# A two-part transformer kernel on one Trainium2 core: its norms taken chunk by chunk

## The reference

```python
def rms_norm(x, g):
    y = x * rsqrt(mean(square(x), axis=-1) + EPS)      # EPS = 1e-6
    return y * g

for layer in range(2):
    h = rms_norm(x, norm_mix_g[layer])
    x = x + (mixer_ab if layer == 0 else mixer_rglru)(h, ...)
    h = rms_norm(x, norm_ffn_g[layer])
    x = x + hierarchical_moe(h, ...)
x = rms_norm(x, norm_final_g)
for i in range(2):
    x = x + attention(rms_norm(x, ln1_g_2[i]), ...)
    x = x + ffn(rms_norm(x, ln2_g_2[i]), ...)
return rms_norm(x, final_g_2)
```

## Time and profile before

| | us |
|---|---|
| median of 3 runs | 2907.57 |
| lowest, highest | 2907.46, 2908.96 |
| the profiled execution, by its own time | 2907.38 |
| its span in the trace | 2906.1 |
| mean granted clock of TensorE | 0.952 |
| busy: PE, PEld, DVE, ACT, POOL | 2752.5, 1905.8, 1198.4, 898.2, 358.9 |

### The profile page before, as it was taken

The page is one execution under the profiler, slowest core; times in us unless marked ns, Lnnn a source line. Parts: engine busy times, 40 slices in busy tenths (PEclk is TensorE's granted clock), DMA queues, the critical chain, the costliest instruction groups (busy, mean ns, idle before and its releaser), DMA issues. The chain is left out here.

```text
span 2906.1 us, 36407 instructions
## 1 busy us (share of the span) xinstructions
PE 2752.5 (95%) x14944; PEld 1905.8 (66%) x14944; DVE 1198.4 (41%) x2253; ACT 898.2 (31%) x1596; POOL 358.9 (12%) x197
## 2 busy tenths in 40 slices
PE   7988999999878899999979999999999999999998
PEld 5874445444656544544467767788887776788887
DVE  2543223223645222322236652552443674245254
ACT  3431111111463110111154543442334454343233
POOL 3200000000330000000020011222122001122112
PEclk9989999999988999999989978999999996899999
DMA  5147999998315799999822011223231201123312
GB/s 201 61 177 302 398 405 406 396 406 340 102 44 195 293 401 408 403 401 405 320 76 73 30 59 44 79 96 102 73 107 56 75 16 58 44 87 103 101 59 80
DMA packets 134825, 543.60 MB, mean 187 GB/s; under 512 B 14592, under 2 KB 26112, under 8 KB 85376
## 3 DMA queue, kind: packets, MB, share of 16 engines
q1 hardware_dynamic: 126976, 536.41, 47.8%
q10 hardware_dynamic: 7680, 4.81, 0.6%
HBM read 539.09 MB, written 2.10 MB: 186 GB/s over the span
## 5 line engine op out<-in xcount | busy, mean ns | idle before, releaser
L484 PE MATMUL ps<-w,w 128*128 128x512 f32 x3360 | 771.0, 391 | 16.4 <-DVE w L430 9.1
L484 PEld LDWEIGHTS ps<-w,w 128*128 128x128 f32 x3360 | 634.2, 189 | 150.6 <-DVE w L430 9.7
L256 POOL TENSOR_TENSOR w<-w,w 128x1024 fp32r<-128x1024 f32 (+3 forms) x139 | 330.2, 2384 | 2294.9 <-ACT w L248 2294.9
L486 PE MATMUL ps<-w,w 128*128 128x512 f32 (+2 forms) x2256 | 498.9, 383 | 27.0 <-ACT w L556 16.0
L486 PEld LDWEIGHTS ps<-w,w 128*128 128x128 f32 x2256 | 417.8, 192 | 105.8 <-ACT w L556 16.3
L1124 PE MATMUL ps<-w,w 128*64 128x512 f32 x2048 | 451.6, 594 | 1.8 <-issue 1.8
L248 ACT ACTIVATE w<-w 128x1024 fp32r<-128x1024 f32 (+3 forms) x260 | 252.6, 1001 | 481.0 <-PE ps L484 254.8
L256 DVE TENSOR_TENSOR w<-w,w 128x1024 fp32r<-128x1024 f32 (+3 forms) x121 | 180.7, 1498 | 456.1 <-ACT w L248 454.3
L1124 PEld LDWEIGHTS ps<-w,w 128*64 128x64 f32 x2048 | 145.9, 137 | 285.5 <-issue 285.5
L1356 DVE TENSOR_TENSOR X<-ps,X 128x512 f32<-128x512 f32 x256 | 164.1, 683 | 222.0 <-PE ps L1160 221.1
L1146 PE MATMUL ps<-w,w 128*64 128x512 f32 x1024 | 226.8, 595 | 0.8 <-ACT w L1201 0.8
(11 more groups left out here) (231 smaller groups left out, 2296.4 us busy)
## 6 DMA issues: line engine op xcount, KB each, us to landing
w<-in_moe_w_gate SPq DMA_DIRECT2D x128, 1024.0 KB, 10.2
w<-in_moe_w_up SPq DMA_DIRECT2D x128, 1024.0 KB, 12.8
w<-in_moe_w_down SPq DMA_DIRECT2D x128, 1024.0 KB, 8.0
w<-in_w_up SPq DMA_DIRECT2D x40, 1024.0 KB, 5.1
w<-in_w_down SPq DMA_DIRECT2D x20, 1024.0 KB, 5.0
w<-in_w_in SPq DMA_DIRECT2D x16, 1024.0 KB, 5.0
w<-in_ab_w_in SPq DMA_DIRECT2D x10, 1024.0 KB, 6.5
w<-in_c_w_in SPq DMA_DIRECT2D x8, 1024.0 KB, 5.3
```

The costliest lines, as they stand in the source:

```text
L256: up(self.wlo[self.low[s][0]], lane.e.tensor_tensor(lo, raw, hi.bitcast(F32), ALU.subtract))
L484: ins = pe.matmul(bank[:, :], wp[:, k, P * o:P * o + P], ap(k0 + k), start=first, stop=stop)
L486: ins = pe.matmul(bank[:, 0:width], ap(k0 + k)[:, P * o:P * o + P], wp[:, k, :], start=first, stop=stop)
```

## The change

The change takes each norm in smaller pieces and starts it earlier:

- the squares of a stage's last product are summed by column halves (`scalar_last_product`): the first half of all four chunks during the last product, the second half behind each chunk's last addition, with a root for each chunk; the sum of the first half enters the root as its bias;
- VectorE scales each chunk behind the next chunk's addition (`vector_last_product`), in the stage before, and the last chunk in two halves; in `moe(0)` two chunks are scaled ahead of chunk 3's additions, in `moe(1)` none;
- the scaled rows lie in fixed places (`XN_`, `HF_`), free at that time;
- TensorE takes the banks of the transposes one by one, so that it waits for each only where it writes it, and waits for halves of chunk 3;
- `tensor_product` runs over input blocks outside and banks inside, and waits for each block by itself;
- the gain of the middle norm comes with the weight units (`plan_middle`), and ScalarE issues four small transfers for the attention at the start of the middle norm; the middle norm is a stage of its own;
- the roots at the start and at the end of the experts are for chunks 0 and 1, then 2, then 3;
- behind the experts only VectorE waits for the roots.

```diff
+    XN_ = (at(8192, 4, 1024), at(20480, 4, 1024))
...
+    def norm_of_rows(XN):
+        def apply(c):
+            if c == 0:
+                mark["xn"] = xn.n
+            w = D if c < NT - 1 else D // 2
+            for j in range(0, D, w):
+                up(xn, dve.tensor_scalar(XN[:, c, j:j + w], X[:, c, j:j + w], SM[:, c:c + 1], None, ALU.mult))
+        return apply
...
     def tensor_norm_features(XN):
-        bs = [banks.take(bf) for _ in range(KD)]
+        bs = []
         for chunks in (range(NT - 1), (NT - 1,)):
             for k in range(KD):
+                if not chunks[0]:
+                    bs.append(banks.take(bf))
                 for c in chunks:
-                    PE.wait_ge(xn, c + 1)
+                    PE.wait_total(xn, mark["xn"] + (c + 1 if c < NT - 1 else NT + k // (KD // 2)))
...
-            ready(k0 + nk)
             hi, lo = (x.rearrange("p (k n) -> p k n", k=nk) for x in W.need(s, PE))
-            for o, bank in zip(outs, bs):
-                for k in range(nk):
+            for k in range(nk):
+                ready(k0 + k + 1)
+                last = end and k == nk - 1
+                for o, bank in zip(outs, bs):
...
+    def scalar_last_product(key, tail):
+        done = len(bx.banks) - 2 * NT
+        steps = W.steps(key)
+        for i, (h, _, _) in enumerate(steps[:len(steps) - tail]):
+            W.hi(h + SPLITS)
+            if i == 0:
+                for c in range(NT):
+                    S.wait_total(bx.free, done + c + 1)
+                    square(X[:, c, 0:512], 512, SM[:, 88 + c:89 + c])
+                S.wait_total(sq, sq.n)
+                S.wait_total(ss, up(ss, act.activation(SM[:, 88:92], SM[:, 88:92], ACT.Identity, bias=ONE[:, 2:3],
+                                                       scale=1.0 / D)))
+        for c in range(NT):
+            S.wait_total(bx.free, done + NT + c + 1)
+            square(X[:, c, 512:D], 512, SM[:, c:c + 1])
+            scalar_roots(c, 1, D, SM[:, 88 + c:89 + c])
+
+    def vector_last_product(key, tail, apply):
+        steps = W.steps(key)
+        for h, _, _ in steps[:len(steps) - tail]:
+            W.lo(h + SPLITS, V)
+        for c in range(NT):
+            vector_add_chunk(1, c)
+            if c:
+                vector_norm(apply, ((c - 1, 1),))
+        vector_norm(apply, ((NT - 1, 1),))
...
+            for c in range(3):
+                vector_combine(c)
+            if next_norm:
+                vector_norm(next_norm, ((0, 2),))
+            vector_combine(3)
+            if next_norm:
+                vector_norm(next_norm, ((2, 1), (3, 1)))
...
         for lane in (PE, S, V, G, SP):
             lane.wait_ge(n_ready, 1)
-            lane.wait_ge(bx.free, 8 * PAIRS)
-            lane.wait_total(rt, rt.n)
-            lane.wait_ge(bdown.free, 2 * PAIRS)
+        V.wait_total(rt, rt.n)
...
+    def plan_middle():
+        W.add("fn", [(1, D, A["norm_final_g"].partition_broadcast(P).unsqueeze(1))], split=False)
```

More of the change, by code:

```diff
@@ L395, in vector_roots, with vector_norm @@
         vstep(dve.reciprocal(a, a))
-    def vector_norm(apply):
-        for c0, n in ((0, NT - 1), (NT - 1, 1)):
+    def vector_norm(apply, groups):
+        for c0, n in groups:
             vector_roots(c0, n)
@@ L487, in tensor_product @@
                                             start=first, stop=stop)
-                if end:
-                    W.consumed_at[s] = (kind.full, up(kind.full, ins))
+                    if last:
+                        W.consumed_at[s] = (kind.full, up(kind.full, ins))
             if not end:
@@ L571, in evacuate, with vector_add_chunk, vector_out @@
             for c in range(NT):
-                bank = bx.next(V)
-                x = X[:, c, 512 * n:512 * n + 512]
-                up(bx.free, dve.tensor_tensor(x, bank[:, :], x, ALU.add))
-        return evacuate
-    def vector_out(key):
-        for n in range(2):
-            vector_product((key, n), vector_add_to_x(n), TAIL * n)
+                vector_add_chunk(n, c)
+        return evacuate
+    def vector_add_chunk(n, c):
+        bank = bx.next(V)
+        x = X[:, c, 512 * n:512 * n + 512]
+        up(bx.free, dve.tensor_tensor(x, bank[:, :], x, ALU.add))
+    def vector_out(key, apply):
+        vector_product((key, 0), vector_add_to_x(0))
+        vector_last_product((key, 1), TAIL, apply)
     def scalar_squares(ready):
@@ L1367, in vector @@
             vector_route()
-            for p in range(PAIRS + 1):
-                now, before, after = p < PAIRS, p > 0, p + 1 < PAIRS
-                if before:
+            for p in range(PAIRS):
+                if p:
                     vector_combine(0)
-                if now:
-                    vector_hidden(p)
-                if before:
+                vector_hidden(p)
+                if p:
                     vector_combine(1)
                     vector_combine(2)
-                if after:
+                if p + 1 < PAIRS:
                     vector_gather(p + 1)
-                if now:
-                    vector_slots(p)
-                if before:
+                vector_slots(p)
+                if p:
                     vector_combine(3)
@@ L1849, in vector @@
         def vector():
-            vector_norm_features(gain, XN, late)
+            vector_norm_features(gain, late)
             vector_product(("mla", i))
@@ L2064, in vector @@
                 for n in range(2):
[L2065 removed]
+                    if m0 and n:
+                        vector_last_product(("fd", i, m0, n), FFN_TAIL, next_norm)
+                    else:
+                        vector_product(("fd", i, m0, n), vector_add_to_x(n))
         def gpsimd():
@@ L2112, in program @@
         plan_ffn(i)
-    def nothing():
-        pass
-    def load_fn_att():
-        load_final("norm_final_g")
-        load_att(0)
     sync_start()
```

173 lines of the change are left out of this document (95 added, 78 removed).

## The result

| us | before | changed kernel |
|---|---|---|
| median of the first timed runs | 2907.52 (4 runs) | 2878.59 (4 runs) |
| lowest, highest | 2901.32, 2908.96 | 2876.93, 2879.96 |
| span of the profiled execution | 2906.1 | 2875.7 |
| TensorE busy in it | 2752.5 | 2737.2 |
| TensorE idle in it (span less busy) | 153.6 | 138.5 |

The ratio is 0.9904, with a 95% interval of 0.9887 to 0.9921: 28.9 us faster, where 19.6 were forecast and 26.6 was the far end of the range. A second set of six runs of the changed kernel had a median of 2878.13, against 2908.34 for the kernel before on the same chip.

A forecast was written before the change was run, and what follows sets the result against it. TensorE was taken as the bound almost everywhere, leaving its idle time and matmul pace. Gains of 20.45 us, less 2.8 for bank order, plus 2.0 for the clock, gave 19.65, so 2888.0 us; range 2881 to 2897.

The forecast's parts named there:

- Dense seams: Three dense seams: only chunk 2's scaling remains behind the last addition, so transposes start 1.3 us earlier each, 3.9 together.
- Into the experts: Two seams into the experts: earlier scalings let TensorE restart 3.3 us sooner each, 6.6 together.
- Out of the first experts: Seam behind the first experts: two chunks scaled before chunk 3's additions, so the bulk of transposes starts 2.2 us earlier.
- Middle: Middle norm: the gain comes with the weight queue, its 5.16 us wait goes, and TensorE's bulk restarts 1.5 us earlier.
- End: Last norm: only chunks 2 and 3 remain to scale behind the last additions, 2.35 us gained.
- Start: Kernel's start: the first two chunks are scaled before the third's root, 1.35 us gained.
- Single features: Products wait for one feature, not two: three output products gain 0.65 us each, the recurrent one 0.6; sum 2.55.
- Order of banks: Narrow groups of two feed-forward stages: later banks delay GpSimd's low part, costing 1.4 us each, minus 2.8 together.
- (1): Rival, dense matmuls: more bank changes slow TensorE; over 22 ns each, chance 0.03; a 5 to 10 us loss, 0.07.
- (2): Rival, seams: lower-clock stretches stay as frequent and new waits open two more, 2890 to 2894 us; chance 0.2.
- (3): Rival: the clock gives +4 to +8 us and the narrow groups don't wait, 2880 to 2884 us; chance 0.1.
- The clock: Eight seams: shorter idling should leave fewer lower-clock stretches on TensorE, +2.0 us, bounds -4 and +8.

The follow-up runs named there:

- e9: Changed kernel with chunk 3's two additions at the end of moe(0) back ahead of the first two scalings: 2875.65 us.
- e7: Changed kernel with the middle norm's gain fetched by ScalarE's queue at the start of that norm instead of with the weights: 2881.80 us.
- e1: Changed kernel with products again running over banks outside and the step's two blocks inside, waiting for both blocks: 2881.16 us.
- e2: Changed kernel with only the last step of a product run bank by bank again, blocks outside in all other steps: 2876.51 us.
- the second pair: Changed kernel and kernel before, each traced once more without edits: 2878.13 us (6 runs) and one execution of 2903.99 us.
- e6: Changed kernel with VectorE's scalings behind all four last additions again at the two seams into the experts alone: 2888.84 us.
- e8: e2 with a product's banks taken one by one, each just ahead of its first matmul: 2859.70 us.
- e5: Changed kernel with VectorE's scalings behind all four last additions again at the three dense seams alone: 2886.76 us.
- e4: Changed kernel with scalings behind all four last additions again at the dense seams, the seams into the experts and the end: 2899.16 us.
- e10: Changed kernel with the edits of e8 and e9 together: 2856.32 us, 0.9835 of the kernel before.

## Why the prediction was wrong

The direction was right and the size was not: the time lies 2.4 us below the range. By the prediction's own steps, from the first pair of traces:

- *Dense seams.* Predicted 1.3 each; the bulk starts 2.95 - 1.61 = 1.34 earlier. Right.
- *Into the experts.* Predicted 3.3 each. Addition to restart took 8.45 and takes 193.40 - 188.55 = 4.85, so 3.6. Right, a little small.
- *Out of the first experts.* Predicted 2.2, measured 6.95 - 5.37 = 1.6. The two scalings ahead of chunk 3's additions took 2.31 us in place of the 1.42 that the earlier trace rows gave, and the additions waited behind them; e9 shows that this step of the change costs 1.2 us at its own seam. What is left of the gain I put down to the earlier root and the missing branch; no run parts the two. The step failed by pricing a move at the duration that the scaling had in another place: the first of the two began while GpSimd still made a low part. (The kernel before varies here: 6.95 in its first trace, 742.10 - 734.00 = 8.10 in its second.)
- *Middle.* Predicted 1.5, measured 14.68 - 12.59 = 2.1. All of it lies ahead of the reciprocal: from there to the bulk it takes 7.92 us where it took 7.87. The mechanism was right (e7, with the gain late, lost 3.7), the size 0.6 short: 0.3 because VectorE came 4.67 us behind the last matmul where I had 1464.1 - 1459.13 = 4.97, since the last root was 0.3 later and 0.67 passed behind it instead of the 1.3 taken over from the other experts' seam, and 0.3 because the scalings took 7.92 where I had 8.2.
- *End.* Predicted 2.35; 4.59 - 2.19 = 2.40. Right. *Start.* Predicted 1.35; the bulk starts at 13.76 against 15.26, so 1.5. Right.
- *Single features.* Predicted 2.55. The waits of features turned back fell by 2.0 and the recurrent one by 0.8, 2.8 together. Right as waits; e1 against e2 shows 4.7 in time.
- *Order of banks.* Predicted minus 1.4 in each narrow pair of ffn; 1.27 measured at the place and for the reason named, and e2 removes it. Right.
- *Rivals.* (1) A change of bank costs nothing that these rows show: 130.84 us for 576 matmuls with either order. (2) and (4) are out, the clock gave more and the seams moved as forecast. (3) comes nearest, but one of its two conditions did not hold: the narrow groups did wait.
- **The clock.** Predicted +2.0 with bounds of -4 and +8. Here is the failed step. TensorE is busy for 15.3 us less in the first pair of traces and for 4.6 us less in the second pair (2744.8 against 2740.2), so no single pair of traces measures it; their mean is 10.0. The times agree: 28.9 gained, of which the steps above explain 4.0 + 7.2 + 1.6 + 2.1 + 1.5 + 2.4 + 2.8 - 2.5 = 19.1. Some 10 us are left for the clock, above my upper bound. This is a difference of medians: against the three groups of the kernel before it would be some 4, 10 and 16.

The sum without the clock, 17.65, is thus right to 1.5 us, in part by luck: out of the first experts it was 0.6 too high, in the middle 0.6 too low. What I did with the clock was to treat it as chance: eight seams, each of which "could win or lose" a stretch, with a small mean. The mean is not small. Over fourteen traces a dense seam's window loses up to 1.4 us less when its idle time falls from some 5.4 to 4.5 us, and nothing at all at 2.4. The prediction had even said that shorter idling leaves fewer such stretches, and then priced that at a quarter of a microsecond a seam. And the one row that I had for the range, 0.50 over 3 us of transposes, was a price without a frequency: the other seams of the same trace would have given it (0.93, 0.86 and 0.86 over three windows).

What stays open: how the 10 us divide between the dense seams (4.3 to 4.7), the experts' seams (e6 lost 2.6 to 3.2 beyond its idle time), the single features (about 2, if e1 is read so) and the rest. The transposes at the start took 4.75 us where they took 6.06, at a granted clock that the profile gives as 1.00 in both. That is no part of the change: over the fourteen traces they took 4.75 to 6.23 us with either kind of kernel, 5.97 in the changed kernel's second trace. And the 1.00 can't be taken at its word there, since the same 30 took 3.50 us at 1.00 in the dense seams.

## What to carry to other kernels

Where TensorE stands still for some microseconds between two long busy pieces, count the idle time and then add to it what the lower clock takes afterwards, from the granted clock over all like seams of the trace, not from one. In this kernel that made a microsecond of idle time worth 1.1 (e7), 1.3 (e8), 1.4 (e6) and up to 2 (e5). And a wait for all banks of a group ahead of its first matmul is such a place: taking them one by one brought 17 us here, more than half of what the whole change did.

## What the runs showed that I had not expected

- Idle time and clock can trade places within one program: the two traces of the kernel before differ by 4.4 us of idle time and 7.7 of busy time, and by 3.3 in the span.
- The timed runs of the kernel before scatter from 2898.55 to 2916.15, those of the changed kernel from 2876.93 to 2879.96, and those of e8 over 2.1 us. The scatter does not follow the mean clock, though: e4, at 0.954 to 0.955, repeats within 2.5 us over 12 runs, and e10, at 0.958 to 0.962, only within 6.4.
- Transposes run faster at the higher clock: 30 of them in 3.50 us at a granted 1.00, in 5.16 with three microseconds of 0.50 among them.
- One kind of scaling (128 x 1024, rows by a column) took 0.75 us in all places of the changed kernel's trace but one. The one that began at 728.75 in the changed kernel, beside a low part of GpSimd's that went on to 729.85, took 1.65. The line of L415 gives shortest, median and longest (the shortest are halves):

```profile
L415 DVE TENSOR_SCALAR w<-X,SM x30: 480/750/1653, 11.4 to 2501.2; 128x1024 f32<-128x1024 f32 x18, 128x512 f32<-128x512 f32 x12
```

  That the two engines disturb each other was not tried by a run of its own.
